# Sample attention on one Trainium2 core: ten key tiles per sequence instead of twelve, a 32-group load for the joined piece of the values, and cached keys that the host lays out turned

## The chip, the cores and the metric

The kernel runs on one core of a Trainium2 chip, as one program. The metric is the device time of one execution in microseconds (us), less is better. A core has five engines that run their own instruction streams (TensorE: PE; VectorE: DVE; ScalarE: ACT; GpSimd: POOL; SyncE: SP, which here only issues DMAs) and 16 DMA engines. The streams meet at semaphores.

## What is computed

One step of a hybrid decoder layer, for a prompt of 2048 tokens and for 8 running sequences of 8 new tokens each (the samples). The change concerns the attention of the samples alone. Each sequence has 2048 cached keys and values (8 heads of 64) and its own 8 new ones:

```python
DILATED = ((128, 1), (512, 4), (2048, 16))

def dilated_attention_sample(q, kc, vc):          # kc, vc: cache and new rows, W = 2048
    for window, dil in DILATED:
        j = jnp.arange(window // dil + 1)
        idx = W + ti[:, None] - dil * j[None, :]   # 129 positions of each token
        kg, vg = kc[:, idx], vc[:, idx]
        s = jnp.einsum('bthd,btjhd->bthj', q, kg)
        mx = jnp.max(s, axis=-1, keepdims=True)
        p = jnp.exp(s - mx)
        ...
    return combine_by_denominator(outs, lses)
```

The three windows are joined by their denominators, which is one softmax in which a position counts once for each window that has it. The kernel does that with one additive mask, the logarithm of the count. Tokens 0 to 7 need, of the cache, the positions whose remainder by 16 is 0 to 7 (over all 2048) and, for the two short windows, positions of the last 512.

## The kernel before

The program has four stages, one after the other with a barrier of all engines between them: `project` (projections), `mix_prompt` (attention and recurrence of the prompt), `mix_sample` (the same for the samples), and `project_out` with `mlp`. The change is in `mix_sample` and in the two places of `mix_prompt` that load keys ahead for it (sequence 0 into `k_first`, sequence 1 into `k_second`).

In `mix_sample` a sequence b has twelve tiles of 128 cached positions, and the 64 new rows of all sequences as a thirteenth (`KT = 13`, `OLD = 12 * P`). Eight tiles are the positions 16i + r, r below 8: partition i gets eight rows of 2 KB that lie together, 16 KB in all. Four tiles are the last 512 positions, four rows or 8 KB in a partition. `load_window` issues the two DMAs of that, for keys (`load_k`, L2023 and L2024) and for values (`load_v`). There are two buffers for the keys (`kin`: `k_first`, `k_second`) and two for the values (`vin`).

Per sequence there are two halves. `first_half(b)`:

- `keys`: TensorE turns each of the twelve tiles, 4 transposes of 128x128 for the four pairs of heads, into one of three PSUM banks (L2469). ScalarE copies the even tiles into `kT` (L2257), VectorE the odd ones (L2326).
- `scores`: for each group of four tiles 4 matmuls with 512 columns of `kT` (L2482), in two PSUM banks by turns, and 4 for the new keys. In the profile a float32 matmul of this kind is two records. The order on TensorE is turn group 0, turn group 1, scores 0, turn group 2, scores 1, scores 2, scores of the new keys.
- `masked`, `maxed` on VectorE add the mask and take the row maximum (L2338, L2344); `exps` on ScalarE takes the exponential over all 1600 columns (L2263).

`second_half(b)`: TensorE turns the probabilities (L2506, L2508), ScalarE and VectorE copy them into `pT` (L2270, L2364, L2366), TensorE multiplies them with the values (13 tiles of 4 matmuls, L2522; called PV below), and VectorE scales the result into `osb` (L2378).

Each engine runs first_half(0), first_half(1), second_half(0), first_half(2), second_half(1), and so on up to second_half(7). Between them lie the recurrence of the samples (a load and a store of its state by POOL's queue, `in_state_C` and `out_C_sample`; its products L2563 and L2532) and the opening of the next stage: loads of `w_out` in four parts (L1802), of `parts` and `mix` (L1806, L1807), their rounding on POOL, ScalarE and VectorE, the first combination on VectorE (`first_weights`, called `between` in second_half(6)), and on TensorE, ahead of PV(7), the products of the first row tile (`first_tile`, L1816 and L292 to L294).

The order of the DMAs is that of SP's stream:

```python
for b in range(DEC_B - 1):
    if b + 2 < DEC_B:
        sp.wait_ge(s["turned"], T.turned("k", b, 11))
        load_k(b + 2)
    if b == 5:
        sp.wait_ge(s["fin"], 16 * 3)
        sp.wait_ge(s["C_out"], 16 * MH)
        ...
        O.load(sp, 0)
        O.load_w(sp, 0)
    if b:
        sp.wait_ge(s["summed"], b)
    load_v(b + 1)
```

After load_v(6) follow the three other parts of `w_out` and O.load(1), then load_v(7). `fin` counts three small stores that SP issues after load_v(5). POOL waits for the turned keys of sequence 0 before it loads the state, and for those of sequence 6 before it rounds `w_out` into the place of `k_first`.

Of the kernel before, what the change touches and what calls it, by code (L numbers as in the profile page):

```python
# [13 lines left out]
P = 128  # L14
# [9 lines left out]
AW = H * HD  # L24
# [1223 lines left out]
def mix_prompt(K):  # L1248
# [12 lines left out]
    with ExitStack() as ctx:  # L1261
# [99 lines left out]
        def _(sp):  # L1361
# [28 lines left out]
            for g in range(T.count + 6):  # L1390
# [27 lines left out]
            sp.wait_ge(s["next_in"], 16 * (2 + SAMPLE_ROWS))  # L1418
# [525 lines left out]
KT = 13  # L1944
OLD = 12 * P
KEYS = OLD + NS
QW = 32


def sample_tables():  # L1950
# [4 lines left out]
    pos = np.concatenate([16 * p + r for r in range(8)] + [WB - 512 + 4 * p + c for c in range(4)]  # L1955
                         + [WB + np.arange(DEC_T)])[None, :]
    back = WB + t - pos
    n = OLD + DEC_T
    part16 = np.zeros(n, bool)
    part16[0:8 * P] = True  # L1960
    new = np.zeros(n, bool)
    new[OLD:] = True
    d16 = (back >= 0) & (back % 16 == 0) & (back <= 2048) & (part16 | new)
    d4 = (back >= 0) & (back % 4 == 0) & (back <= 512) & ~part16
    d1 = (back >= 0) & (back <= 128) & ~part16
# [18 lines left out]
class Turns:  # L1984
# [6 lines left out]
    def __init__(self):  # L1991
        order = [("q", 0, 0), ("new", 0, 0)]
        for b in range(DEC_B + 1):
            if b < DEC_B:
                order += [("k", b, x) for x in range(12)]
# [25 lines left out]

def load_window(sp, dst, cache, b, landed):
    sp.dma_start(dst[:, 0:8], cache[b].rearrange("(i r) c -> i r c", r=16)[:, 0:8]).then_inc(landed, 16)  # L2023
    sp.dma_start(dst[:, 8:12], cache[b, WB - 512:WB, :].rearrange("(i r) c -> i r c", r=4)).then_inc(landed, 16)  # L2024
# [37 lines left out]
def mix_sample(K):  # L2062
# [9 lines left out]
    with ExitStack() as ctx:  # L2072
# [15 lines left out]
        sb("kin_home", [P, 12, AW])  # L2088
        later = [12 * AW]
# [6 lines left out]
        vin = [front("vin0", 12, AW), sb("vin", [P, 12, AW])]  # L2096
        vnew = sb("vnew", [NS, AW])
        kT = sb("kT", [P, 2, PAIRS, 512])
        knT = sb("knT", [P, PAIRS, NS])
        pr = front("pr", 2, KEYS)  # L2100
        qs, knew, mq, mkk, n32 = K.qs, K.knew, K.mq, K.mkk, K.n32
        qz = front("qz", DEC_B, PAIRS, QW)
        pT = front("pT", KT, P)
# [18 lines left out]
        pT_last = kin[1][:].rearrange("p x c -> p (x c)")[:, 12 * AW - KT * P:].rearrange("p (x r) -> p x r", r=P)  # L2122

        def pt(b):
            return pT[:] if b + 1 < DEC_B else pT_last
# [74 lines left out]
        def _(pool):  # L2200
# [15 lines left out]
            pool.wait_ge(s["turned"], T.turned("k", 0, 11))  # L2216
# [12 lines left out]
            pool.wait_ge(s["turned"], T.turned("k", 6, 11))  # L2229
# [5 lines left out]
        def rows(x):  # L2235
            return P if x < 12 else NS

        @block.scalar
        def _(act):
# [11 lines left out]
            def keys(b):  # L2251
                for x in range(0, 12, 2):
                    n = 3 * b + x // 4
                    act.wait_ge(s["turned"], T.turned("k", b, x))
                    if x % 4 == 0 and n >= 2:
                        act.wait_ge(s["scores"], 4 * ((n - 2) // 3) + (n - 2) % 3 + 1)
                    A(kT[:, n % 2, :, P * (x % 4):P * (x % 4 + 1)], bank[T.bank("k", b, x)][:].rearrange("p (h c) -> p h c", h=PAIRS),  # L2257
                      ACT.Copy).then_inc(s["copied_a"], 1)

# [5 lines left out]
            def probs(b):  # L2265
                for i in (0, 2):
# [3 lines left out]
                    A(pt(b)[:, 4 * i:4 * i + 4], bank[T.bank("p", b, i)][:].rearrange("p (x r) -> p x r", x=4),  # L2270
# [15 lines left out]
            keys(0)  # L2286
# [5 lines left out]
            keys(1)  # L2292
            probs(0)
            exps(1)
            for b in range(2, DEC_B):
                keys(b)
# [16 lines left out]
        def _(dve):  # L2313
# [6 lines left out]
            def keys(b, ci):  # L2320
                for x in (4 * ci + 1, 4 * ci + 3):
                    n = 3 * b + ci
                    dve.wait_ge(s["turned"], T.turned("k", b, x))
                    if x % 4 == 1 and n >= 2:
                        dve.wait_ge(s["scores"], 4 * ((n - 2) // 3) + (n - 2) % 3 + 1)
                    v.tensor_copy(kT[:, n % 2, :, P * (x % 4):P * (x % 4 + 1)],  # L2326
                                  bank[T.bank("k", b, x)][:].rearrange("p (h c) -> p h c", h=PAIRS)).then_inc(s["copied_d"], 1)

            def masked(b, c):
                p, n = b % 2, 4 * b + c  # L2330
                w = 512 if c < 3 else NS
# [5 lines left out]
                table = mask[:, 512 * c:512 * (c + 1)] if c < 3 else mask_new[:, b]  # L2337
                v.tensor_tensor_reduce(pr[:, p, 512 * c:512 * c + w], bank[SC[n % 2]][:, 0:w], table, 1.0, 2 * NEG,  # L2338
# [7 lines left out]
            def first_half(b, groups=None):  # L2346
                for ci in range(3):
                    keys(b, ci)
# [9 lines left out]
            def probs(b):  # L2358
                for i in (1, 3):
# [5 lines left out]
                    else:  # L2365
                        ins = v.tensor_copy(pt(b)[0:NS, 12], bank[T.bank("p", b, i)][0:NS, 0:P])  # L2366
# [88 lines left out]
        def _(pe):  # L2455
# [1495 lines left out]
```

## Time and profile before

| | |
|---|---|
| runs | 2785.67, 2789.16, 2790.73 us (median 2789.16) |
| the profiled execution: span from first to last instruction | 2790.8 us |
| the profiled execution: device time | not given apart; its span lies at the upper end of the three runs |
| PE busy | 2667.3 us (96%) |
| DVE, ACT, POOL busy | 1806.6 us (65%), 1075.5 us (39%), 692.4 us (25%) |
| mean granted TensorE clock | 0.986 |
| first instruction of `mix_sample` to its last product | 1076.8 us to 1246.4 us |

Times of the trace are counted from the start of the span. A window row gives, for a stretch, the busy time and number of instructions of each engine, the granted TensorE clock as a share of 2.4 GHz, the busy share of the 16 DMA engines and what they moved.

### The profile page before, as it was taken

The page shows a single profiled execution, that of the slowest core. Times are in us where ns is not written, and L with a number is a line of the kernel's source. Part 1 is how long each engine was busy: PE and PEld are TensorE (multiplying, and loading weights), DVE is VectorE, ACT ScalarE, POOL GpSimd, SP SyncE. Part 2 cuts the span into 40 slices and gives each one's busy share as a digit, 9 for nine tenths or more (in the row PEclk, how much of TensorE's full clock was granted, in tenths as well). Part 3 has the DMA queues.
Part 4 walks back from the last instruction along what each step waited for, and adds up shares of the span by engine and source line. Part 5 has one row for each costly group of instructions (what it writes and reads, how often), then busy time and mean ns, then how long its engine had stood idle before and what let it go on. Part 6 is the DMA issues. An engine that isn't in the chain of part 4 may idle for free. (4 is left out here: it accounts for less than half of the span.)

```text
span 2790.8 us, 45736 instructions
## 1 busy us (share of the span) xinstructions
PE 2667.3 (96%) x17331; PEld 2256.3 (81%) x17331; DVE 1806.6 (65%) x3848; ACT 1075.5 (39%) x1975; POOL 692.4 (25%) x585
## 2 busy tenths in 40 slices
PE   7999999999899998989989999899999999999997
PEld 6888888878777776768877888799998888778886
DVE  6722566333688885567667676755655766887778
ACT  4312332010566774333346555555553211221113
POOL 1167212120245453112210000100002434333332
PEclk9999999999999999989999999999999999999999
DMA  5367543254454547967846777778869777786672
GB/s 184 140 214 265 198 145 143 107 178 139 138 174 155 172 142 290 399 263 261 303 164 209 269 270 269 263 269 298 278 234 335 271 243 255 265 310 225 220 266 87
DMA packets 342705, 628.68 MB, mean 225 GB/s; under 512 B 38431, under 2 KB 241315, under 8 KB 326742
## 3 DMA queue, kind: packets, MB, share of 16 engines
q1 hardware_dynamic: 273132, 530.24, 54.8%
q10 hardware_dynamic: 68218, 91.51, 9.1%
q0 software_dynamic: 1152, 4.19, 0.4%
q8 instruction: 130, 2.13, 0.3%
q14 instruction: 73, 0.60, 0.1%
HBM read 455.36 MB, written 237.61 MB: 248 GB/s over the span
## 5 line engine op out<-in xcount | busy, mean ns | idle before, releaser
L3573 DVE TENSOR_TENSOR mlp_acc<-mlp_acc,bank 128x512 f32<-128x512 f32 x440 | 299.6, 685 | 143.4 <-PE bank L2861 137.1
L2859 PE MATMUL bank<-mlp_wd,mlp_u_hi 128*128 128x512 f32 x896 | 350.5, 391 | 8.9 <-DVE mlp_acc L3573 5.1
L2861 PE MATMUL bank<-mlp_wd,mlp_u_lo 128*128 128x512 f32 x896 | 349.2, 390 | 0.0
L2860 PE MATMUL bank<-mlp_wd,mlp_u_hi 128*128 128x512 f32 x896 | 349.1, 390 | 0.0
L3342 ACT ACTIVATE mlp_u_hi<-mlp_u_raw 128x768 fp32r<-128x768 f32 x126 | 113.1, 945 | 445.4 <-POOL mlp_u_raw L3210 445.0
L2859 PE MATMUL bank<-mlp_h_hi,mlp_wu_hi 128*128 128x272 f32 x896 | 259.3, 289 | 9.3 <-DVE mlp_h_lo L3431 4.8
L2860 PE MATMUL bank<-mlp_h_lo,mlp_wu_hi 128*128 128x272 f32 x896 | 258.8, 289 | 0.0
L2861 PE MATMUL bank<-mlp_h_hi,mlp_wu_lo 128*128 128x272 f32 x896 | 257.9, 288 | 0.0
L292 PE MATMUL p_bank<-p_w_hi,p_hT_hi 128*128 128x512 f32 x640 | 250.4, 391 | 5.2 <-DVE p_stage L836 5.1
L294 PE MATMUL p_bank<-p_w_hi,p_hT_lo 128*128 128x512 f32 x640 | 249.1, 389 | 0.0
L293 PE MATMUL p_bank<-p_w_lo,p_hT_hi 128*128 128x512 f32 x640 | 249.1, 389 | 0.0
L3205 POOL TENSOR_TENSOR mlp_u_raw<-mlp_u_raw 128x256 f32<-128x256 f32 x64 | 50.3, 787 | 718.3 <-DMA mlp_u_raw<-u 718.3
L2859 PEld LDWEIGHTS bank<-mlp_wd,mlp_u_hi 128*128 128x128 f32 x896 | 168.6, 188 | 48.6 <-issue 10.9
L832 DVE TENSOR_TENSOR p_bank<-p_bank,p_rot 128x128 f32<-128x128 f32 x85 | 25.4, 299 | 265.9 <-PE p_bank L294 234.7
L2861 PEld LDWEIGHTS bank<-mlp_wd,mlp_u_lo 128*128 128x128 f32 x896 | 168.5, 188 | 35.3
L2860 PEld LDWEIGHTS bank<-mlp_wd,mlp_u_hi 128*128 128x128 f32 x896 | 168.7, 188 | 34.4
L1508 ACT ACTIVATE mx_probs<-mx_probs,mx_part 128x256 f32<-128x256 f32 (+1 forms) x384 | 143.4, 451 | 96.8 <-DVE mx_part L1587 96.8
L2859 PEld LDWEIGHTS bank<-mlp_h_hi,mlp_wu_hi 128*128 128x128 f32 x896 | 169.4, 189 | 10.7 <-DVE mlp_h_lo L3431 5.7
L2859 PE MATMUL bank<-mlp_g_hi,mlp_wu_hi 128*128 128x512 f32 x444 | 173.4, 391 | 3.7 <-DVE mlp_made L3444 2.1
L2860 PE MATMUL bank<-mlp_g_lo,mlp_wu_hi 128*128 128x512 f32 x448 | 175.3, 391 | 0.0
L2861 PE MATMUL bank<-mlp_g_hi,mlp_wu_lo 128*128 128x512 f32 x444 | 172.8, 389 | 0.0
L2860 PEld LDWEIGHTS bank<-mlp_h_lo,mlp_wu_hi 128*128 128x128 f32 x896 | 169.2, 189 | 0.0
(448 smaller groups left out, 6104.4 us busy)
## 6 DMA issues: line engine op xcount, KB each, us to landing
mlp_wd<-wd SPq DMA_DIRECT2D x31, 2048.0 KB, 8.1
mlp_wd<-wd SPq DMA_DIRECT2D x32, 1536.0 KB, 7.3
mlp_u_raw<-u SPq DMA_DIRECT2D x256, 128.0 KB, 2.4
out_win_k_sample<-in_cache_k SPq DMA_DIRECT2D x48, 680.0 KB, 8.9
out_win_v_sample<-in_cache_v SPq DMA_DIRECT2D x48, 680.0 KB, 9.6
mlp_wu_raw<-in_w_up SPq DMA_DIRECT2D x31, 1024.0 KB, 6.0
p_w_raw<-in_w_tok SPq DMA_DIRECT2D x10, 2048.0 KB
wd<-mlp_un_hi SPq DMA_DIRECT2D x21, 896.0 KB, 4.5
```

Of the source, the lines that this page charges most:

```text
L292: nc.tensor.matmul(out, ah, bh, start=(k == 0), stop=False)
L293: nc.tensor.matmul(out, ah, bl, start=False, stop=False)
L294: ins = nc.tensor.matmul(out, al, bh, start=False, stop=(k == n - 1))
L832: v.tensor_tensor(rot_a, ps[:, :, 0:ROT], tab(0, ROT), ALU.mult)
L1508: ins = A(p_, p_, ACT.Exp, bias=part[a][:, n % 2, 2 * c + e, HD + 1:HW])
L2859: nc.tensor.matmul(out, ah, bh, start=fresh and k == 0, stop=False, skip_group_check=not fresh)
L2860: nc.tensor.matmul(out, ah, bl, start=False, stop=False, skip_group_check=not fresh)
L2861: ins = nc.tensor.matmul(out, al, bh, start=False, stop=k == n - 1, skip_group_check=not fresh)
L3205: g_.tensor_tensor(r[:, 3], r[:, 2], r[:, 5], ALU.add).then_inc(u_sums, 1)
L3342: A(u_hi[b][:, k], u_raw[b][:, k], ACT.Copy).then_inc(u_hi_ready, 1)
L3573: v.tensor_tensor(a, a, b[:], ALU.add).then_inc(summed, 1)
```

## The change

- Tiles: the positions of the last 512 whose remainder by 16 is below 8 are already in the eight first tiles. The four late tiles become two, with remainders 8 to 15 only. `KT` is 11, `OLD` 1280; the mask counts all windows over all columns.
- Values: `load_window` now takes for the late piece, of each 16 rows of the last 512, the second eight: 32 groups of 4 partitions, 2 rows (4 KB) in a partition.
- Keys: the host passes a further input, `cache_kt`, with the keys of the ten tiles turned (for each sequence 128 x 4 x 1280). One DMA brings 20 KB to each partition. `keys` goes on all three engines, the matmuls of `scores` read the loaded buffer itself. The third group of scores has 256 columns.
- What waited for the turned keys of a sequence (SP's next load of keys, POOL's two places) waits for its third group of scores.
- The places of all buffers stay; the mask, the exponential (1344 columns) and the PV (11 tiles) get shorter. The copy of the caches into the outputs still reads `cache_k` and `cache_v`.

```diff
@@ mix_prompt, sync
-                    load_window(sp, K.k_second, K.ins["cache_k"], 1, K.k_second_in)
+                    load_keys(sp, K.k_second, K.ins["cache_kt"], 1, K.k_second_in)
...
-                    load_window(sp, K.k_first, K.ins["cache_k"], 0, s["next_in"])
+                    load_keys(sp, K.k_first, K.ins["cache_kt"], 0, s["next_in"])
@@
-KT = 13
-OLD = 12 * P
+WT = 10
+KT = WT + 1
+OLD = WT * P
@@
+def sample_key_columns(cache):
+
+    p = np.arange(P)
+    late = WB - 512 + 16 * (p // 4) + 8 + 2 * (p % 4)
+    pos = np.concatenate([16 * p + r for r in range(8)] + [late + y for y in range(2)])
+    return cache[:, pos, :].reshape(DEC_B, OLD, H // 2, P).transpose(0, 3, 2, 1)
+
+
+def load_keys(sp, dst, turned, b, landed):
+    sp.dma_start(dst[:], turned[b]).then_inc(landed, 16)
+
 def load_window(sp, dst, cache, b, landed):
     sp.dma_start(dst[:, 0:8], cache[b].rearrange("(i r) c -> i r c", r=16)[:, 0:8]).then_inc(landed, 16)
-    sp.dma_start(dst[:, 8:12], cache[b, WB - 512:WB, :].rearrange("(i r) c -> i r c", r=4)).then_inc(landed, 16)
+    sp.dma_start(dst[:, 8:WT], cache[b, WB - 512:WB, :].rearrange("(i z a y) c -> z i a y c", z=2, a=4, y=2)[1]).then_inc(landed, 16)
@@ mix_sample, sync
-                load_window(sp, kin[b % 2], K.ins["cache_k"], b, k_in[b % 2])
+                load_keys(sp, kin[b % 2], K.ins["cache_kt"], b, k_in[b % 2])
...
-                    sp.wait_ge(s["turned"], T.turned("k", b, 11))
+                    sp.wait_ge(s["scores"], 4 * b + 3)
@@ gpsimd
-            pool.wait_ge(s["turned"], T.turned("k", 0, 11))
+            pool.wait_ge(s["scores"], 3)
...
-            pool.wait_ge(s["turned"], T.turned("k", 6, 11))
+            pool.wait_ge(s["scores"], 4 * 6 + 3)
@@ scalar: keys(b) and its calls go
-            def keys(b):
-                for x in range(0, 12, 2):
...
@@ vector: keys(b, ci) and its call go
-            def keys(b, ci):
-                for x in (4 * ci + 1, 4 * ci + 3):
...
-                w = 512 if c < 3 else NS
+                w = min(512, OLD - 512 * c) if c < 3 else NS
@@ tensor
-            def keys(b, ci):
-                p = b % 2
-                for x in range(4 * ci, 4 * ci + 4):
-                    dst = open_group("k", b, x)
-                    for c in range(PAIRS):
-                        ins = tp(dst[:, P * c:P * (c + 1)], kin[p][:, x, P * c:P * (c + 1)], ident[:])
-                    ins.then_inc(s["turned"], 1)
...
-                w = 512 if ci < 3 else NS
-                if ci < 3:
-                    after(pe, T.out("k", b, 4 * ci + 2))
-                    after(pe, T.out("k", b, 4 * ci + 3))
+                w = min(512, OLD - 512 * ci) if ci < 3 else NS
...
-                    src = kT[:, (3 * b + ci) % 2, c, :] if ci < 3 else knT[:, c, :]
+                    src = kin[b % 2][:, c, 512 * ci:512 * ci + w] if ci < 3 else knT[:, c, :]
```

## Rows read from the trace of the kernel before

**Rows 1.** Span and mean granted TensorE clock of the core.
```profile
core 0: 2790.8 us, clock 0.986
```

**Rows 2.** Windows: stretch, length; PE, PEld, DVE, ACT, POOL busy; clock, DMA share, GB/s.
```profile
1120.00:1140.00 20.00, 19.58 (x246) 16.55 (x243) 13.02 (x36) 6.39 (x10) 0.00 (x0) 1.00 1.00 424
1140.00:1160.00 20.00, 19.58 (x246) 14.84 (x238) 13.37 (x39) 6.69 (x12) 3.75 (x2) 1.00 0.95 381
1180.00:1200.00 20.00, 16.45 (x196) 12.17 (x195) 7.50 (x18) 6.39 (x10) 2.06 (x2) 0.83 1.01 419
```

**Rows 3.** Timeline of TensorE, 1165 to 1224 us: start, length, instruction, [idle before, releaser].
```profile
1165.75 4.49 PE L2522 MATMUL bank<-sm_vin,sm_pT 128*32 128x128 f32 x96 [2.45 <-issue]
...
1205.28 3.88 PE L2469 MATMUL bank<-ident,k_second 128*128 128x128 f32 x32
1209.09 1.07 PE L2482 MATMUL bank<-sm_kT,sm_qz 128*32 128x512 f32 x8
...
1214.16 1.53 PE L2506 MATMUL bank<-ident,sm_pr 128*128 128x128 f32 x12
1215.62 0.43 PE L2508 MATMUL bank<-ident,sm_pr 128*64 128x128 f32 x2
1216.47 2.83 PE L2522 MATMUL bank<-sm_vin,sm_pT 128*32 128x128 f32 x96 [0.42 <-ACT sm_pT L2270]
1219.23 0.42 PE L2522 MATMUL bank<-sm_vnew,sm_pT 64*32 64x128 f32 x8
```

**Rows 4.** Groups of instructions in `mix_sample`: times, busy us, mean ns, idle before.
```profile
L2326 DVE COPY sm_kT<-bank 128x512 f32<-128x512 f32 x48 | 33.1, 691 | 20.0 <-PE bank L2469 19.8
L2257 ACT ACTIVATE sm_kT<-bank 128x512 f32<-128x512 f32 x48 | 28.7, 597 | 51.4 <-PE bank L2469 51.3
```

**Rows 5.** Single DMAs: duration and start of issue, time to landing (keys 3, keys 5, w_out 1 to 3).
```profile
L2024 SPq DMA_DIRECT2D k_second<-in_cache_k x1: 433/433/433, 1099.8 to 1099.8; - x1
...
DMA to landing us min/median/max: 22.6/22.6/22.6
...
L2024 SPq DMA_DIRECT2D k_second<-in_cache_k x1: 432/432/432, 1140.0 to 1140.0; - x1
...
DMA to landing us min/median/max: 11.8/11.8/11.8
...
L1802 SPq DMA_DIRECT2D out_w_raw<-in_w_out x3: 432/442/447, 1189.6 to 1190.6; - x3
...
DMA to landing us min/median/max: 17.0/19.0/21.1
```

**Rows 6.** Windows by what the DMAs carried, and one after a pause of TensorE.
```profile
1078.30:1122.40 44.10, 40.51 (x427) 29.79 (x427) 22.06 (x52) 17.60 (x33) 11.53 (x13) 0.97 1.00 389
1122.40:1151.80 29.40, 28.56 (x396) 23.04 (x393) 19.66 (x56) 10.69 (x18) 3.75 (x2) 1.00 1.00 417
1158.00:1170.30 12.30, 9.85 (x149) 7.56 (x152) 6.76 (x23) 3.06 (x5) 3.57 (x4) 0.86 0.92 338
1165.70:1170.20 4.50, 4.45 (x100) 4.26 (x100) 0.02 (x1) 0.00 (x0) 0.00 (x0) 0.62 0.98 349
```

**Rows 7.** DMA issues, 1050 to 1260 us: times, KB each, median us to landing.
```profile
k_second<-in_cache_k SPq DMA_DIRECT2D x4, 2048.0 KB, 10.5
...
k_second<-in_cache_k SPq DMA_DIRECT2D x4, 1024.0 KB, 12.6
...
out_C_sample<-sm_Cs POOLq DMA_DIRECT2D x4, 512.0 KB, 10.3
```

**Rows 8.** Timeline of all engines, the end of the stage.
```profile
1222.81 0.35 DVE L2378 TENSOR_SCALAR sm_osb<-bank,sm_st 128x128 f32<-128x128 f32 x1
1223.08 0.68 DVE L2364 COPY k_second<-bank 128x512 f32<-128x512 f32 x1
...
1224.05 0.63 PE L1816 MATMUL bank<-ident,out_ma 128*128 128x128 f32 x4 [2.58 <-DVE k_second L2366]
...
1246.04 0.42 PE L2522 MATMUL bank<-sm_vnew,k_second 64*32 64x128 f32 x8
```

More of the change, by code:

```diff
@@ L1941, in sum_up @@
         v.tensor_tensor(w[:, 5], w[:, 4], w[:, 1], ALU.subtract).then_inc(self.wu_t, 1)
-KT = 13
-OLD = 12 * P
+WT = 10
+KT = WT + 1
+OLD = WT * P
 KEYS = OLD + NS
+HOME = 12
 QW = 32
@@ L1954, in sample_tables @@
     p = np.arange(P)
-    pos = np.concatenate([16 * p + r for r in range(8)] + [WB - 512 + 4 * p + c for c in range(4)]
-                         + [WB + np.arange(DEC_T)])[None, :]
+    late = WB - 512 + 16 * (p // 4) + 8 + 2 * (p % 4)
+    pos = np.concatenate([16 * p + r for r in range(8)] + [late + y for y in range(2)] + [WB + np.arange(DEC_T)])[None, :]
+    assert len(set(pos[0].tolist())) == pos.size
     back = WB + t - pos
     n = OLD + DEC_T
[L1959 to L1965, printed above, removed]
+    assert pos.shape[1] == n
+    d16 = (back >= 0) & (back % 16 == 0) & (back <= 2048)
+    d4 = (back >= 0) & (back % 4 == 0) & (back <= 512)
+    d1 = (back >= 0) & (back <= 128)
     count = d16.astype(np.float32) + d4 + d1
@@ L1993, in __init__ @@
         for b in range(DEC_B + 1):
-            if b < DEC_B:
-                order += [("k", b, x) for x in range(12)]
             if b:
@@ L2087, in mix_sample @@
         assert -(-nc.sbuf_base // 32) * 32 == K.front_at + 4 * TOP
-        sb("kin_home", [P, 12, AW])
-        later = [12 * AW]
+        sb("kin_home", [P, HOME, AW])
+        later = [HOME * AW]
         def front(name, *shape):
@@ L2120, in mix_sample @@
         SC, PV, ML = (3, 4), 5, (6, 7)
-        pT_last = kin[1][:].rearrange("p x c -> p (x c)")[:, 12 * AW - KT * P:].rearrange("p (x r) -> p x r", r=P)
+        pT_last = K.place("sm_pT_last", TOP + HOME * AW - KT * P, [P, KT, P])
         def pt(b):
-            return pT[:] if b + 1 < DEC_B else pT_last
+            return pT[:, 0:KT] if b + 1 < DEC_B else pT_last
         def pv(b):
@@ L2235, in rows @@
         def rows(x):
-            return P if x < 12 else NS
+            return P if x < WT else NS
         @block.scalar
@@ L2249, in _ @@
                 act.wait_ge(K.hb_out[p], 16 * (NCH // 2))
-            def keys(b):
-                for x in range(0, 12, 2):
[L2253 to L2258, printed above, removed]
             def exps(b):
@@ L2285, in _ @@
             own.mark(ins)
-            keys(0)
             exps(0)
@@ L2291, in _ @@
             own.mark(ins)
-            keys(1)
             probs(0)
@@ L2295, in _ @@
             for b in range(2, DEC_B):
-                keys(b)
                 probs(b - 1)
@@ L2318, in bc @@
                 return ap.rearrange("p (h a) -> p h a", a=1).broadcast_to([NS, MH, w])
-            def keys(b, ci):
-                for x in (4 * ci + 1, 4 * ci + 3):
[L2322 to L2327, printed above, removed]
             def masked(b, c):
                 p, n = b % 2, 4 * b + c
-                w = 512 if c < 3 else NS
+                w = min(512, OLD - 512 * c) if c < 3 else NS
                 dve.wait_ge(s["scores"], n + 1)
@@ L2336, in masked @@
                     dve.wait_ge(s["turned"], T.turned("p", b - 2, 3))
-                table = mask[:, 512 * c:512 * (c + 1)] if c < 3 else mask_new[:, b]
-                v.tensor_tensor_reduce(pr[:, p, 512 * c:512 * c + w], bank[SC[n % 2]][:, 0:w], table, 1.0, 2 * NEG,
+                at = 512 * c if c < 3 else OLD
+                table = mask[:, at:at + w] if c < 3 else mask_new[:, b]
+                v.tensor_tensor_reduce(pr[:, p, at:at + w], bank[SC[n % 2]][:, 0:w], table, 1.0, 2 * NEG,
                                        ALU.add, ALU.max, st[:, p, c:c + 1]).then_inc(s["masked"], 1)
@@ L2347, in first_half @@
                 for ci in range(3):
-                    keys(b, ci)
                     if ci:
@@ L2486, in first_half @@
                 if b:
-                    pe.wait_ge(k_in[b % 2], 32 * ((b + 1) // 2))
+                    pe.wait_ge(k_in[b % 2], 16 * ((b + 1) // 2))
                 for ci in range(3):
-                    keys(b, ci)
                     if ci:
@@ L2503, in second_half @@
                     if i < 3:
-                        for k in range(4):
+                        for k in range(min(4, WT - 4 * i)):
                             x = 4 * i + k
@@ L2522, in second_half @@
                         ins = mm(bank[pv(b)][QW * c:QW * (c + 1), 0:2 * HD], pt(b)[0:w, x, QW * c:QW * (c + 1)],
-                                 vin[p][:, x, P * c:P * (c + 1)] if x < 12 else vnew[:, P * c:P * (c + 1)],
+                                 vin[p][:, x, P * c:P * (c + 1)] if x < WT else vnew[:, P * c:P * (c + 1)],
                                  start=(x == 0), stop=(x == KT - 1))
@@ L3760, in sb @@
             return ctx.enter_context(K.nc.sbuf_tensor("shared_" + name, shape, F32))
-        K.k_first, K.k_second = K.place("k_first", 0, [P, 12, AW]), K.place("k_second", TOP, [P, 12, AW])
+        K.k_first, K.k_second = K.place("k_first", 0, [P, H // 2, OLD]), K.place("k_second", TOP, [P, H // 2, OLD])
         K.C = sb("C", [P, MH, MD + 1])
```

19 lines of the change are left out of this document (11 added, 8 removed).

## Prediction

> **What bounds the kernel now.** I read the span first [rows 1]: one core, a TensorE clock of 0.986, so there is little disturbance to explain away. The page puts TensorE at 96% of the span, but that is a mean over four stages, and the change touches one. So I next read windows inside `mix_sample` [rows 2]: TensorE is busy 19.58 of 20 us in two of them, and the 16 DMA engines are busy for 0.95 to 1.00 of the same stretches at 381 to 424 GB/s. Two resources look full at once. Which one ends last is seen where a sequence's data lands and where it is used. Keys 3 landed at 1099.8 + 22.6 = 1122.4 us, keys 5 at 1140.0 + 11.8 = 1151.8 us [rows 5]. Part 1 of `w_out` landed at 1189.6 + 17.0 = 1206.6 us [rows 5]; values 6 stand directly ahead of it in SP's queue, so they landed about the 2.5 us of its 1.05 MB before, near 1204, yet PV(6) starts at 1216.47 [rows 3]. So the loads ran some 12 us ahead at the end, and TensorE set the time; but only 12 us ahead. That margin, and not TensorE's share, decides what the change is worth.
>
> **What TensorE loses.** 384 transposes of keys at 3.88 / 32 = 0.121 us [rows 3]: 46.6 us. The third scores group has half its columns: 8 times half of 1.07 us [rows 3], 4.3. Two tiles fewer in the transposes of the probabilities: 16 at 1.53 / 12 = 0.128, 2.0. PV: 8 x 2 tiles x 8 records at 2.83 / 96 = 0.0295 [rows 3], 3.8. Together 56.7 us. ScalarE and VectorE lose 28.7 and 33.1 us of copies [rows 4]; both spent their time waiting for TensorE [rows 4], so this gives nothing by itself. The new waits of SP and POOL on the third scores group come later than the turned keys by about one or two groups of scores, but the scores themselves now start at once: behind SP's wait stand the next keys and values, and those are far back in a full queue anyway.
>
> What is left on TensorE for a sequence: scores 2.5 x 1.07 + 0.3 = 3.0 us, probabilities 1.3 + 0.43 + 0.42 = 2.1, PV 2.4 + 0.4 = 2.8; 7.9 us, plus the recurrence in three of the sequences.
>
> **What the DMAs keep.** A sequence's keys or values are 2048 + 1024 KB = 3.146 MB before [rows 7] and 2560 KB = 2.621 MB after. Keys and values of a sequence need 5.24 MB at 0.42 MB/us = 12.5 us (the window that carries nothing else has 417 GB/s [rows 6]; by the landings of keys 3 and 5, 12.58 MB in 29.4 us, it is 0.428 [rows 5]). That is more than 7.9 us. So the loads become the bound, and the stage is to be summed in bytes:
>
> 1. From load_v(0) at 1078.3 to keys 3. Before: v0, k2, v1, k3 12.58 MB, state 2.10, masks 1.05, rows 0.4, 16.1 MB in 44.1 us, 0.366 MB/us (the window itself has 389 GB/s, since some of values 2 is in it [rows 6]). After: 10.49 + 2.10 + 0.92 + 0.4 = 13.9 MB, 38.0 us: keys 3 land at 1116.3.
> 2. v2, k4, v3, k5, v4, k6, v5, k7: 20.97 MB at 0.42, 49.9 us. Store of the state (4 x 512 KB [rows 7]) and the three small stores, 2.25 MB; where that store ran the rate was 338 GB/s [rows 6], I take 0.36: 6.2 us. Keys 7 land at 1172.4.
> 3. O.load(0), `w_out` 0 and v6: 2.12 + 2.62 MB at 0.42, 11.3 us: values 6 land at 1183.7.
> 4. PV(6) starts there instead of at 1216.5 [rows 3]: 32.8 us earlier.
> 5. From PV(6) on, the tail is the next stage's opening and not bound by sample loads: 30.0 us before, to 1246.5 [rows 8]. Two corrections. VectorE's `first_weights` lay between TensorE's last PV and its own copies of the probabilities, so that TensorE sat idle for 2.58 us before L1816 [rows 8]; now it is done while PV(6) waits for its values: -2.6. And PV(6) starts after a pause. After such a pause of 2.45 us PV(3) took 4.49 us instead of 2.83, at a granted clock of 0.62, partly the lower level of 1.2 GHz [rows 3, 6]. The same factor of 1.6 on PV(6) and on the ten transposes behind it, less their two tiles: +1.9. Net -0.7.
>
> Sum: 32.8 + 0.7 = 33.5 us. 2790.8 - 33.5 = 2757.3 us of span. The profiled execution is 1.6 us over the median of the runs, so 2789.16 - 33.5 = 2755.7, which I round to **2756 us**. The stages behind start from the same state and only shift.
>
> **Is the queue always fed?** At the time when keys b land, v(b-1), k(b+1) and v(b) are issued already, since each waits only for work on sequence b-1 or b-2. The tight place is b = 5: SP waits for `fin`, three small stores queued behind v5, before it issues O.load(0), `w_out` and v6. By the sum v5 lands about 1166 and the stores some 2 us later, while k7 keeps the engines busy to 1172. Margin about 4 us; if it is gone, each us more costs one. In the tail, `w_out` 2 and 3 land 5 and 8 us after v6, O.load(1) 10 us, v7 16 us; they are used some 5, 13, 13 and 26 us after PV(6) starts. Covered, `w_out` 2 just so. The smaller first loads in `mix_prompt` lie under a stage that TensorE orders: 0, with bounds of -1 and +0.5 us.
>
> **Costs that no row shows.** Late values in 32 groups with 4 KB pieces: below, the rate of rows 6 (0.524 MB, 1.25 us); above, the lowest rate there, 338 GB/s (1.55 us), over seven loads +2 us. I take the first, as the same rows of 2 KB come from the same cache. Keys in 20 KB rows from one DMA: they are as long as or longer than any now loaded; the same rate, bounds -0.2 and +1.2 us each (338 GB/s), over the six of the stage -1 to +7. Matmuls reading the loaded buffer instead of `kT`: both are SBUF, 0.
>
> The Trainium skill has a rule that bears on the first of these ("DMA: Bandwidth & Descriptors", section "Why a DMA increments its semaphore by 16 and not by 1", at "How many engines (k)"): a DMA is spread over the largest number up to 16 that divides the slowest dimension of both sides. Here the sides have 32 and 128, which gives 16 and the 1.25 us above; by the four partitions of a group it would be 4. No row of before has this shape.
>
> **Rivals.**
>
> - *TensorE stays the bound, at its lower clock.* Pauses for each sequence might hold it at 1.2 GHz: then the 7.9 us of a sequence become about 15, above the 12.5 of the loads. Over the six sequences from keys 3 on that is 15 us, gain 18, **2771 us**. For it: 0.62 after one pause [rows 6]. Against it: once TensorE is the slower one it has no pauses, and in the windows without pauses the clock is 1.00 [rows 2]. The skill's page "TensorE: Matmul & The Clock Gate" (HAM oscillation) tells of a kernel whose short bursts between DMA waits each began at the low clock; by that this rival would hold. 0.10.
> - *The 32-group load runs on few engines* (the other sign). One engine moves 0.42 / 16 = 0.026 MB/us, so n engines need 20 / n us for a piece instead of 1.25, and the later loads need those engines too. Seven pieces precede PV(6). With four engines +26 us, 2782; with three +38, slower; with one +131, **2887 us**. It decides from 6 us for a piece on. Against it: nothing but the shape, 32 is a multiple of 16. 0.04 for slower, 0.03 for the case of four.
> - *TensorE's saving counts in full*, 57 us, 2732: needs the loads to hide. They can't: 41.9 MB must land before PV(6), at the best 0.428 MB/us 98 us after 1078.3, so PV(6) not before 1176 and the gain not above 41. A better rate in step 1 than the 0.366 gives up to 5 us, near **2750**; 0.10 for below 2751.
> - *The queue runs dry* at b = 5 or at the start: 3 to 8 us, **2762**; 0.08.
>
> **Chances and range.** My forecast, loads as the pace and 2751 to 2761: 0.65. Range 2747 to 2771: above it the few engines (0.07) and part of the low-clock case, below it little. Faster by over 0.2% (which is about what a measurement of this kernel can tell from no change): 0.94; within it 0.01; slower 0.05.
>
> **What would show it.** The DMA share stays at 1.00 from 1078 to past 1185 at 400 GB/s and more, while TensorE's busy share falls to about 0.6 to 0.8 with granted clocks below 1 (right), or stays above 0.9 (the first rival). PV waits on landings of `sm_vin` in most sequences, and PV(6) starts with the landing of values 6, near 1184. TensorE's gap before L1816 is under 1 us. A late-values DMA that lands over 3 us after the piece issued 0.4 us before it shows the second rival. Wrong outright would be a DMA share under 0.9 in the middle with TensorE waiting: then something issues too late.

## The result, and the profile after

The changed kernel took 2770.9 us (median of 4 runs, 2770.26 to 2774.66), the kernel before beside it 2788.56 us (4 runs, 2785.67 to 2790.73). The ratio is 0.994 with a 95% interval of 0.9927 to 0.9954. Measured again later, five runs gave 2770.24 us and 0.9932 (0.9918 to 0.9945). The change makes the kernel faster by 17.7 us, 0.6% (18.8 us in the later series). The forecast was 33 us: the direction held, and about half of the gain is missing.

First the core, as in [rows 1]:

```profile
core 0: 2768.4 us, clock 0.982
```

The windows of `mix_sample` after the change (columns as in [rows 2]; the last one is a short stretch inside the third):

```profile
1080.00:1100.00 20.00, 12.89 (x180) 6.56 (x180) 7.58 (x31) 4.53 (x8) 7.46 (x6) 0.91 1.00 399
1100.00:1120.00 20.00, 7.73 (x50) 7.76 (x51) 0.00 (x0) 0.00 (x0) 0.00 (x0) 0.58 1.02 411
1120.00:1140.00 20.00, 18.72 (x291) 14.48 (x290) 13.18 (x47) 5.05 (x10) 3.74 (x2) 1.00 0.72 274
1140.00:1160.00 20.00, 16.77 (x219) 10.67 (x221) 13.00 (x49) 4.26 (x7) 3.57 (x4) 0.91 1.00 401
1160.00:1180.00 20.00, 13.61 (x245) 7.29 (x237) 5.63 (x21) 2.86 (x6) 0.00 (x0) 0.91 1.02 422
1180.00:1200.00 20.00, 9.20 (x116) 7.53 (x116) 17.79 (x22) 5.38 (x8) 13.63 (x4) 0.71 1.01 419
...
1122.00:1127.00 5.00, 4.54 (x103) 3.70 (x102) 4.00 (x12) 2.38 (x4) 0.00 (x0) 1.00 0.08 28
```

As forecast, the DMA engines are full and TensorE isn't: 12.89, then 7.73 of 20 us. But from 1120 to 1140 the roles are reversed again: TensorE is busy for 18.72 us and the DMA share is 0.72 at 274 GB/s, where before it was 1.00 at 424 [rows 2]. From 1122 to 1127 the DMA engines are nearly idle, at 28 GB/s. The prediction had named a DMA share under 0.9 in the middle as what would prove it wrong. It had added "with TensorE waiting"; here TensorE's long wait lies just before the hole (1097.8 to 1112.3 us), not in it.

TensorE's timeline shows what stands ahead of that hole, and the end of the stage (start, length, instruction, idle before with its releaser):

```profile
1112.27 9.46 PE L2541 MATMUL bank<-sm_Cs,sm_qm 128*64 128x129 f32 x64 [14.49 <-DMA sm_Cs<-in_state_C]
...
1175.48 3.72 PE L2461 MATMUL bank<-k_second,sm_qz 128*32 128x512 f32 x24 [4.61 <-DMA k_second<-in_cache_kt]
...
1186.70 4.49 PE L2500 MATMUL bank<-sm_vin,sm_pT 128*32 128x128 f32 x80 [5.08 <-DMA sm_vin<-in_cache_v]
...
1199.23 1.09 PE L1816 MATMUL bank<-ident,out_ma 128*128 128x128 f32 x4 [5.66 <-DVE sm_pT_last L2356]
...
1221.25 0.42 PE L2500 MATMUL bank<-sm_vnew,sm_pT_last 64*32 64x128 f32 x8
```

Two waits were not in the forecast: 14.49 us for the recurrence's state at L2541 (which is L2563 of before), and 5.66 us before L1816, where it had said under 1 us. Keys 7 and values 6 are waited for (4.61 and 5.08 us), which fits the loads as the pace, and PV(6) then takes 4.49 us, as PV(3) did after its pause before [rows 3]. One sign did not come: PV was to wait for its values in most sequences, and it did so in two, PV(5) for 1.12 us and PV(6).

**The first loss: the state.** The kernel before issued the state's load later and yet did not wait for it:

```profile
L2218 POOL DMA_DIRECT2D sm_Cs<-in_state_C x4: 882/887/1067, 1087.8 to 1090.7; - x4
...
DMA to landing us min/median/max: 12.0/18.6/26.3
```
```profile
1117.07 7.23 PE L2563 MATMUL bank<-sm_Cs,sm_qm 128*64 128x129 f32 x64 [1.25 <-DMA sm_Cs<-in_state_C]
```

The same load after the change:

```profile
L2228 POOL DMA_DIRECT2D sm_Cs<-in_state_C x4: 882/887/1067, 1080.3 to 1083.1; - x4
...
DMA to landing us min/median/max: 13.8/20.9/29.0
```

It was issued 7.5 us earlier, but its last part landed at 1083.1 + 29.0 = 1112.1 us, only 5 us earlier than before (1090.7 + 26.3 = 1117.0), and 4.1 us of that is the whole stage, whose load_v(0) was issued at 1074.19 instead of 1078.34 us. TensorE, with no keys to turn, was there at 1112.27 - 14.49 = 1097.8 us; before it came at 1115.8. The DMA queues of 1080 to 1112 us say why the landing takes so long (packets, MB, share of the 16 engines' time; the first is SP's queue, the second POOL's):

```profile
q1 hardware_dynamic: 889, 10.63, 82.4%
q0 software_dynamic: 576, 2.10, 18.0%
```

POOL's 2.10 MB go beside 10.63 MB of SP's queue and get less than a fifth of the engines. The Trainium skill ("DMA: Bandwidth & Descriptors", section "Queues, rings and completion order") says that each DMA engine takes turns between its queues packet by packet; the trace fits that only roughly, since it isn't one for one: 576 packets against 889, of 3.6 KB against 12 KB.

The wait would be harmless by itself, with the loads as the pace. What counts stands behind it. In TensorE's stream PV(1) comes after the state's products, and SP's load_v(3) waits for PV(1). SP's own issues in the stretch (start, length):

```profile
1092.84 0.33 SPq L2033 DMA_DIRECT2D sm_vin<-in_cache_v  x1
1093.21 0.59 SPq L2034 DMA_DIRECT2D sm_vin<-in_cache_v  x1
1097.30 0.33 SPq L2029 DMA_DIRECT2D k_first<-in_cache_kt  x1
```
```profile
1126.66 0.33 SPq L2033 DMA_DIRECT2D sm_vin<-in_cache_v  x1
```

For 29 us nothing is issued. Keys 4, the last in the queue, are reported landed at 1097.3 + 26.5 = 1123.8 us; the window from 1122 us on shows that next to nothing is moved any more, and the queue is dry until load_v(3).

**The second loss: the end of the stage.** VectorE and POOL, 1182 to 1199 us:

```profile
1182.49 4.51 POOL L1854 TENSOR_TENSOR out_w_lo<-out_w_raw,out_w_hi 128x2048 fp32r<-128x2048 f32 x1
1182.67 4.39 DVE L1868 TENSOR_TENSOR out_st<-out_st,out_pt 128x24 f32<-128x24 f32 x1
...
1191.57 4.84 POOL L1854 TENSOR_TENSOR out_w_lo<-out_w_raw,out_w_hi 128x2048 fp32r<-128x2048 f32 x1
1192.07 4.89 DVE L1892 TENSOR_TENSOR out_prod_first<-out_prod_first 128x512 f32<-128x512 f32 x1
...
1198.26 0.68 DVE L2354 COPY sm_pT_last<-bank 128x512 f32<-128x512 f32 x1
```

VectorE's sum over 24 columns took 4.39 us and ended 0.06 us after the POOL subtraction beside it; its sum over 512 columns took 4.89 us and ended 0.55 us after POOL's, which is about its own length. Before, the same two took:

```profile
1216.69 0.20 DVE L1868 TENSOR_TENSOR out_st<-out_st,out_pt 128x24 f32<-128x24 f32 x1
...
1221.09 0.69 DVE L1892 TENSOR_TENSOR out_prod_first<-out_prod_first 128x512 f32<-128x512 f32 x1
```

POOL's two subtractions had been done by 1213.3 us then. That is 4.2 + 4.2 us on VectorE (and 1.7 more, since its three products between them took 3.59 us beside POOL's cast instead of 1.90), and its copies of the last probabilities, for which TensorE waits, stand behind. The Trainium skill has this ("SBUF — State Buffer", section "SBUF: two separate sides"): a VectorE operation with two inputs in SBUF and a GpSimd operation that reads SBUF need the same pair of ports, and the one that comes first has it for its whole length. The rows agree: VectorE isn't slowed in proportion to its own work. Each sum ends when POOL's instruction is over, or its own length after that.

### The profile page after: what moved, and what is told of

Same layout as the page of the kernel before. It is cut to its first block and busy times, and to the rows that moved or that the text cites. A ratio compares the mean times of both kernels' runs of the same rounds, so it can differ in the third digit from the quotient of the medians.

```text
span 2768.4 us, 44506 instructions
## 1 busy us (share of the span) xinstructions
PE 2615.6 (94%) x16803; PEld 2209.4 (80%) x16803; DVE 1780.3 (64%) x3800; ACT 1045.1 (38%) x1927; POOL 685.4 (25%) x585
## 5 line engine op out<-in xcount | busy, mean ns | idle before, releaser
L3320 ACT ACTIVATE mlp_u_hi<-mlp_u_raw 128x768 fp32r<-128x768 f32 x126 | 113.1, 946 | 446.6 <-POOL mlp_u_raw L3188 446.2
```

Source lines behind the costliest of these rows:

```text
L3320: A(u_hi[b][:, k], u_raw[b][:, k], ACT.Copy).then_inc(u_hi_ready, 1)
```

## The experiments

All ratios are against the kernel before, in the same series; after a median stand its runs' extremes. Since one execution differs from another by some us, the stretch itself was also read from each kernel's timeline, of one execution each:

| kernel | load_v(0) to PV(6), us | PV(6) to the end of PV(7) | both |
|---|---|---|---|
| before | 1078.34 to 1216.47: 138.1 | 30.0 | 168.1 |
| changed | 1074.19 to 1186.70: 112.5 | 35.0 | 147.5 |
| changed, again | 1074.18 to 1187.26: 113.1 | 35.0 | 148.1 |
| the prediction | 105.4 | 29.3 | 134.7 |
| ten tiles alone | 1077.81 to 1197.80: 120.0 | 32.4 | 152.4 |
| turned keys alone | 1076.52 to 1205.16: 128.6 | 34.2 | 162.8 |
| late values plain | 1075.94 to 1189.02: 113.1 | 35.3 | 148.4 |
| state on SP's queue | 1075.65 to 1181.30: 105.7 | 35.0 | 140.6 |
| products behind PV(1) | 1073.15 to 1181.98: 108.8 | 35.0 | 143.8 |
| state at the stage's start | 1079.39 to 1184.48: 105.1 | 35.5 | 140.6 |
| the last two together | 1072.56 to 1182.57: 110.0 | 35.0 | 145.0 |
| POOL's rounding later | 1071.82 to 1182.40: 110.6 | 32.1 | 142.6 |
| it and products behind PV(1) | 1075.19 to 1183.92: 108.7 | 32.8 | 141.6 |
| it and state on SP's queue | 1077.49 to 1183.72: 106.2 | 33.8 | 140.0 |

### The parts of the change

**Ten tiles alone**, the kernel before with these edits (the scores, masks and copies shortened to match, the keys still turned on TensorE):

```diff
-KT = 13
-OLD = 12 * P
+WT = 10
+KT = WT + 1
+OLD = WT * P
@@ load_window
-    sp.dma_start(dst[:, 8:12], cache[b, WB - 512:WB, :].rearrange("(i r) c -> i r c", r=4))
+    sp.dma_start(dst[:, 8:WT], cache[b, WB - 512:WB, :].rearrange("(i z a y) c -> z i a y c", z=2, a=4, y=2)[1])
```

> Ten tiles and the 32-group load of the late values, keys still turned on TensorE. Theory (TensorE sets the time of the kernel before and its loads run only 12 us ahead): each sequence loses 2.2 us of TensorE work (8 transposes of 0.121 us, half a scores group 0.53, two probability transposes 0.25, two tiles of PV 0.47), 17.8 us over eight; some 5 us of it go back because the state load still lands near 1115 us while TensorE comes to it earlier. 2773 to 2779 us, so most of what the whole change gave. Rival (the host's turning is what gave the gain): 2783 us or more.

Measured: 2773.41 us (2770.22 to 2776.46), ratio 0.9948 (0.9935 to 0.9961). In its windows TensorE stays busy, and by 1140 us the DMA share has room:

```profile
1100.00:1120.00 20.00, 19.19 (x242) 15.55 (x243) 7.77 (x25) 5.36 (x9) 0.00 (x0) 1.00 1.00 398
...
1140.00:1160.00 20.00, 17.45 (x249) 13.55 (x242) 13.57 (x42) 5.75 (x12) 3.76 (x5) 1.00 0.84 307
```

About three quarters of the measured gain is there with the tiles alone: 13.5 us by the medians, of 17.7 and 18.8.

The trace of this kernel shows one thing more. TensorE still turns the keys, and yet it waits 5.05 us before L1816, since VectorE's first combination already meets POOL's subtraction (its first sum, over 8 columns, ends with POOL's instruction at 1201.04 us):

```profile
1196.49 4.55 POOL L1854 TENSOR_TENSOR out_w_lo<-out_w_raw,out_w_hi 128x2048 fp32r<-128x2048 f32 x1
...
1197.62 3.45 DVE L1866 TENSOR_TENSOR out_st<-out_pt 128x8 f32<-128x8 f32 x1
```

**Turned keys alone**, the changed kernel with twelve tiles:

```diff
-WT = 10
+WT = 12
@@ sample_key_columns
-    late = WB - 512 + 16 * (p // 4) + 8 + 2 * (p % 4)
-    pos = np.concatenate([16 * p + r for r in range(8)] + [late + y for y in range(2)])
+    pos = np.concatenate([16 * p + r for r in range(8)] + [WB - 512 + 4 * p + c for c in range(4)])
```

> Keys turned by the host, but twelve tiles for keys and values as before. Theory (the loads are the pace once TensorE does not turn keys): 6.9 MB more have to land before PV(6) than in the changed kernel, 16 us at 0.42 MB/us, so about 2783 to 2790 us, hardly faster than before although TensorE loses 47 us of work; DMA share near 1.00 through the stage. Rival (TensorE's work counts, the changed kernel was held up only by single waits): 47 us less work shows for at least half, 2765 us or less.

Measured: 2786.18 us (12 runs, 2780.91 to 2791.06), ratio 0.9997 (0.9987 to 1.0008): taking the transposes of the keys from TensorE is worth at most some 4 us by the interval while the loads are as long as before. Its one trace has the stretch to PV(6) shorter by 9.5 us and the end of the stage longer by 4.2. TensorE's longest single waits in the stage (in total, times, longest) are for loads:

```profile
PE bank L2542 <- DMA sm_Cs<-in_state_C: 7.9, 1, 7.9
PE bank L2462 <- DMA k_first<-in_cache_kt: 6.7, 1, 6.7
```

So the tiles shorten both resources and bring most of the gain; the host's turning takes work only from TensorE, and by itself gives next to nothing. It isn't the bytes alone that hold this kernel: the DMA share is 0.79 from 1140 to 1160, so here too loads are issued too late. What the turning is worth depends on that: on top of ten tiles it gives 3 us as the change has it, and 10 us once the load of the state is repaired (2763.67 below, against 2773.41).

**The late values as one plain group.** It settles what the 32 groups cost:

```diff
-    sp.dma_start(dst[:, 8:WT], cache[b, WB - 512:WB, :].rearrange("(i z a y) c -> z i a y c", z=2, a=4, y=2)[1])
+    sp.dma_start(dst[:, 8:WT], cache[b, WB - 256:WB, :].rearrange("(i y) c -> i y c", y=2))
```

> The changed kernel, but the late values come from the last 256 positions, two rows in each of 128 partitions, one plain group (other values than the attention needs; bytes and pieces of 4 KB are the same). Theory (the 32-group form costs nothing by itself: alone it landed 1.2 us behind the large piece): 2769 to 2773 us. Rival (32 groups are spread badly over the engines, over 1 us for each piece): 2763 us or less.

Measured: 2770.3 us (2764.84 to 2776.5), ratio 0.9933 (0.9908 to 0.9957), the same as the changed kernel. In the changed kernel the grouped piece of values 3, issued into the empty queue at 1127.0, landed after 8.2 us, the 2 MB piece issued at 1126.7 after 7.3: 1.2 us apart. In this one the times are 1127.9 + 8.4 and 1127.6 + 7.5, again 1.2 us apart. The prediction's 1.25 us stands, and with it the Trainium skill's rule that was put beside it: 0.524 MB in 1.2 us is the rate of all the engines together. The kernels' times could not decide this alone, with an interval of 7 us to either side; the landings do.

### The state's wait

**The state on SP's queue**, behind values 1, so that it has no second queue beside it:

```diff
@@ sync, behind load_v(b + 1)
+                if b == 0:
+                    by_head = Cs[:].rearrange("p (b h) c -> p b h c", h=MH)
+                    for h in range(MH):
+                        sp.dma_start(by_head[:, :, h, 0:MD], K.ins["state_C"][:, h].rearrange("b d e -> d b e")).then_inc(s["C_in"], 16)
@@ gpsimd: the same four DMAs and their wait for scores 3 go
```

> The changed kernel with the load of the recurrent state issued by SP behind values 1 instead of by POOL. Theory (the state load in POOL's own queue gets about a fifth of the engines' packets beside SP's full queue, lands 29 us after its issue, and TensorE waits 14.5 us for it; in that wait SP issues no new load and the queue runs dry for 4.6 us): it lands in the order in which it is needed, some 6 us behind values 1; TensorE waits under 8 us, the queue never runs dry, values 6 land 4 to 6 us earlier, 2764 to 2767 us. Rival (all is bytes, the order of the loads does not matter): 2770 to 2772 us.

Measured: 2763.67 us (2761.5 to 2766.05), ratio 0.9917 (0.9903 to 0.9931). TensorE still waits 9.9 us for the state, more than the 8 forecast, but the window with the hole is full, and the landing is quicker:

```profile
1120.00:1140.00 20.00, 19.17 (x269) 13.42 (x263) 15.67 (x56) 2.67 (x6) 3.74 (x2) 1.00 1.00 411
```
```profile
L2193 SPq DMA_DIRECT2D sm_Cs<-in_state_C x4: 604/2480/12641, 1083.3 to 1100.1; - x4
...
DMA to landing us min/median/max: 7.0/13.5/19.5
```

**The products moved behind PV(1)**, on TensorE and, for the numerators, on VectorE. The load stays as it is:

```diff
@@ tensor
-            pe.wait_ge(s["act_ml"], 3)
-            ... the wait for C_in and the 64 products
             second_half(1)
+            pe.wait_ge(s["act_ml"], 3)
+            ... the same
@@ vector
-            second_half(1, numerators)
+            second_half(1)
+            numerators()
```

> The changed kernel with the products of the state moved behind second_half(1) on TensorE, and their sums on VectorE too. The state load stays in POOL's queue and lands as late. Theory (what costs is not TensorE's wait but that PV(1) stands behind it, so that SP's load of values 3 is held back and the queue runs dry): the wait stays, the DMA share has no hole near 1122 to 1127 us, 2764 to 2767 us. Rival (TensorE's wait of 14.5 us itself is the loss): 2770 to 2772 us, since the wait is as long.

Measured: 2764.77 us (2762.97 to 2774.17), ratio 0.9929 (0.9912 to 0.9946). The state lands as late as ever (14.5/21.1/29.1 us after its issue), but only 2.26 us are waited for it, so the wait did not stay as the forecast had it, and the rival's condition wasn't met:

```profile
1120.00:1140.00 20.00, 17.07 (x209) 11.93 (x210) 15.83 (x56) 2.67 (x6) 3.75 (x2) 1.00 0.86 350
```
```profile
1110.85 8.89 PE L2543 MATMUL bank<-sm_Cs,sm_qm 128*64 128x129 f32 x64 [2.26 <-DMA sm_Cs<-in_state_C]
```

The hole is smaller and has moved. Values 3 are now issued at 1108.6 us, but the scores of sequence 3 stand behind the products, and SP's load of keys 5 waits for those: it issues nothing from 1109.6 to 1129.5 us.

```profile
1126.00:1132.00 6.00, 5.55 (x64) 3.75 (x67) 5.32 (x22) 1.81 (x3) 3.09 (x2) 1.00 0.55 174
```

One kernel keeps a wait of 9.9 us and one of 2.3 us, and the one with the long wait is no slower: 105.7 us to PV(6), against 108.8 and the changed kernel's 112.5. What counts is how full the window with the hole gets (411, 350 and 274 GB/s), so it is the load held back that costs, and not TensorE's wait. By ratio the gains on the changed kernel (mean of its two, 0.9936) are 5 and 2 us, the second within the noise.

**The state issued by POOL at the stage's start**, without its wait for the scores of sequence 0:

```diff
@@ gpsimd
             g.memset(qm[:], 0.0).then_inc(s["clear"], 1)
+            for h in range(MH):
+                pool.dma_start(by_head[:, :, h, 0:MD], K.ins["state_C"][:, h].rearrange("b d e -> d b e")).then_inc(s["C_in"], 16)
...
-            pool.wait_ge(s["scores"], 3)
-            for h in range(MH): ... the same DMAs
```

> The changed kernel with POOL's load of the state issued at once at the stage's start, behind POOL's three clears, instead of after the scores of sequence 0: some 4 to 5 us earlier. Theory (about a fifth of the packets beside SP's queue, so some 25 us from issue to landing whenever it is issued): it lands 4 to 5 us earlier, TensorE's wait and the hole in the loads shrink by that, 2766 to 2768 us. Rival (it takes its share from keys 2 and values 1, which were late already): 2770 us or more.

Measured: 2763.4 us (2759.23 to 2767.12), ratio 0.9905 (0.9888 to 0.9922), 3 us below the expected range, with 105.1 us to PV(6). The state's wait shrinks, and part of it turns up as a wait for keys 2, which now share the engines with the state; the hole is gone:

```profile
1120.00:1140.00 20.00, 18.72 (x289) 13.68 (x288) 15.23 (x53) 5.05 (x10) 3.75 (x2) 1.00 1.01 423
```
```profile
PE bank L2460 <- DMA k_first<-in_cache_kt: 7.1, 1, 7.1
...
PE bank L2540 <- DMA sm_Cs<-in_state_C: 2.7, 1, 2.7
```

**Two of these together, and the changed kernel again.** The first of these kernels has both edits of the two diffs just shown (early load, products behind PV(1)).

> The state is loaded at the stage's start (alone: 2763) and its products stand behind the PV of sequence 1 (alone: 2765). Theory (both only keep the values' loads from being held back by the state, and the loads are the pace): they don't add, 2761 to 2765; the DMA share stays near 1.00 from 1080 to 1180. Rival (each takes away a wait of its own, 7 and 6 us): they add, 2757 to 2759.

> The changed kernel once more, unedited, beside the two kernels of this call, so that gains of 3 to 8 us over it are read against runs of the same chip. Both theories: 2771 us, ratio 0.993 to 0.995, TensorE's wait for the state near 14 us and its gap before L1816 over 5 us.

Measured: 2765.66 us (2761.92 to 2768.79), ratio 0.9919 (0.9905 to 0.9933), beside the changed kernel's 2770.24 us (2766.21 to 2771.23), 0.9932 (0.9918 to 0.9945). The repairs don't add; with 110.0 us to PV(6) the two are not even as good as the early load alone (105.1). The trace shows part of the reason: as with the products moved alone, SP issues nothing from 1107.8 to 1126.8 us, since keys 5 wait for the scores behind the products, and from 1124 to 1130 the DMA engines move 320 GB/s, with TensorE busy throughout at a granted clock of 0.50, the lower level of 1.2 GHz. How much of the 5 us this explains wasn't tested. The unedited kernel repeats its picture closely, 14.69 us for the state, 5.53 us before L1816, 265 GB/s from 1120 to 1140.

### The end of the stage

**POOL rounds `w_out` only once VectorE's first combination is done:**

```diff
@@ gpsimd
             pool.wait_ge(s["scores"], 4 * 6 + 3)
+            pool.wait_ge(O.mixed, 1)
```

> The changed kernel, but POOL waits for VectorE's first combination before it rounds w_out. Theory (in the changed kernel the two fall together, and two of VectorE's instructions that read two buffers take 4.4 and 4.9 us instead of 0.2 and 0.7, each as long as POOL's 4.5 us subtraction; TensorE waits 5.7 us for what follows on VectorE): both are short again, TensorE's wait before L1816 falls under 1 us, 4 to 5 us faster, 2765 to 2768 us. Rival (the wait comes back as a wait of the products for w_out, since POOL ends 7 us later): 2770 to 2774 us.

Measured: 2769.85 us (2761.49 to 2773.73), ratio 0.9935 (0.9919 to 0.9951): about 1 us better than the changed kernel, which isn't clear of the noise. The forecast of 4 to 5 us missed, and the rival's range is nearer. The profiled execution is the fastest of the six (2761.49 us), so the trace flatters this kernel. In the trace the collision is gone and the wait before L1816 with it, and both come back behind it:

```profile
1178.11 0.20 DVE L1868 TENSOR_TENSOR out_st<-out_st,out_pt 128x24 f32<-128x24 f32 x1
...
1181.98 0.69 DVE L1892 TENSOR_TENSOR out_prod_first<-out_prod_first 128x512 f32<-128x512 f32 x1
...
1191.95 4.53 POOL L1854 TENSOR_TENSOR out_w_lo<-out_w_raw,out_w_hi 128x2048 fp32r<-128x2048 f32 x1
...
1193.45 5.18 DVE L1854 TENSOR_TENSOR out_w_lo<-out_w_raw,out_w_hi 128x2048 fp32r<-128x2048 f32 x1
```
```profile
1189.91 0.63 PE L1816 MATMUL bank<-ident,out_ma 128*128 128x128 f32 x4 [0.42 <-ACT sm_pT_last L2273]
...
1196.54 0.80 PE L292 MATMUL bank<-out_w_hi,out_mT_hi 128*128 128x512 f32 x1 [1.10 <-POOL out_w_lo L1854]
...
1203.59 0.50 PE L292 MATMUL bank<-out_w_hi,out_mT_hi 128*128 128x512 f32 x1 [1.64 <-DVE out_w_lo L1854]
```

From the start of PV(6) to the end of PV(7) it is 32.1 us, against 35.0 in the changed kernel. The forecast's 29.3 plus these two waits (1.10 + 1.64) gives 32.0. So the wait of 5.66 us is freed, and half of it goes back at once.

**This together with the products moved:**

> Both repairs: the products of the state behind second_half(1), and POOL's rounding behind VectorE's first combination. Theory (two separate losses, the first 6 us by its own run, the second 4 to 5): 2759 to 2762 us. Rival (they cover each other): as the first alone, 2764 us or more.

Measured: 2768.24 us (2761.51 to 2770.43), ratio 0.9925 (0.9908 to 0.9942): a miss, the rival's range came. TensorE waits 4.4 us for the low parts of `w_out` (0.7 for POOL's, 3.7 for VectorE's), and the stretch from PV(6) to PV(7) is 32.8 us. The trace, again of the fastest execution, shows 2 us less there than with the products alone; the runs show no difference (ratio 0.9929 there).

**And together with the state on SP's queue:**

> The state loaded by SP's queue behind values 1 (alone: 2764) and GpSimd's rounding of w_out held until VectorE's first combination is done (alone: 2770, 1 us less than the changed kernel). Theory (the second repair gives its time back as a wait for the low part of w_out, as with the products moved, 2768): 2762 to 2766. Rival (the end of the stage still holds some 3 us that a repair without the low part's lateness would free): 2760 or less.

Measured: 2762.21 us (2761.16 to 2763.28), ratio 0.9906 (0.989 to 0.9921). All its runs lie below all of the changed kernel beside it (2766.21 to 2771.23), by 8 us in the medians. It is the fastest median of all, though by ratio level with the state at the stage's start (0.9905); against the state on SP's queue alone (2763.67, 140.6 us of stretch against 140.0) nothing is resolved.

## Why the prediction came out half right

| | predicted | measured |
|---|---|---|
| load_v(0) to keys 3 (step 1) | 38.0 us | 1074.2 to 1111.5: 37.3 |
| keys 3 to keys 7 (step 2) | 56.1 | 1111.5 to 1175.4: 63.9 |
| keys 7 to PV(6) (step 3) | 11.3 | 1175.4 to 1186.7: 11.3 |
| PV(6) to the end of PV(7) (step 5; 30.0 before) | 29.3 | 1186.70 to 1221.67: 35.0 |

Keys 3 and 7 are from their loads (1087.3 + 24.2 and 1158.0 + 17.4 us).

**What held.** The loads become the pace of the stage: DMA share 1.00 or more in five of the six windows from 1080 to 1200, TensorE waiting for keys and values, clocks of 0.58 to 0.91 where it waits. Steps 1 and 3 came out within 0.7 us. The slow PV(6) came too, a little dearer than costed: 4.49 us for 80 records, where 1.6 times the 2.83 us less two tiles is 4.1. The 32-group load cost its 1.25 us, and of the rival in which TensorE stays the bound at its lower clock (2771 us) only the number was hit: where that clock is low, TensorE waits, as with 0.58 from 1100 to 1120 beside a DMA share of 1.02.

**Step 2 failed, by 7.8 us, through "Is the queue always fed?".** The prediction said that v(b-1), k(b+1) and v(b) are issued already when keys b land, and looked for the tight place at b = 5. The tight place was b = 2: load_v(3) waits for PV(1), and PV(1) stands behind the state's products. The wait for the state was not in the sum at all, since the kernel before hid all but 1.25 us of it behind the turning of the keys. What had hidden it was TensorE's own work, and the change removed it. The DMA share below 0.9 in the middle is the sign that the prediction had set for this; with the state on SP's queue, or loaded at the stage's start, the stretch to PV(6) was 105.7 and 105.1 us, where the prediction had 105.4. Step 2 itself, from keys 3 to keys 7, was 56.9 and 55.9 us in these two, against 56.1 predicted: its bytes and rates were right, and the issue of the loads was what failed. By size it is the rival "the queue runs dry, 3 to 8 us", at another place than the two that it named.

**Step 5 failed, by 5.7 us.** "-2.6, `first_weights` is done while PV(6) waits for its values" took VectorE's durations as fixed. It did begin ahead of that PV (1181.9 us), but so did POOL's rounding, which the landing of `w_out` 0 at 1180.4 us released. Before, POOL began it at 1197.9 us and was done 3 us before VectorE began its combination at 1216.3 us. Now VectorE's combination stands behind the landing of keys 7 (1175.4 us) and POOL's rounding behind the next pieces of the same queue, so they meet. That TensorE turns keys 7 would not keep them apart: with ten tiles alone it does, and they meet as well (5.05 us before L1816). The two-input sums were blocked, 4.2 us twice, and the wait before L1816 became 5.66 us, not under 1. With POOL held back it was 0.42 us: the step's own reasoning was right but for the engine beside it. That this frees only about half of it in the trace, and nothing clear of the noise in the runs, was not foreseen either: POOL's and VectorE's low parts of `w_out` are late next.

**The sum.** 33.5 - 7.1 (load_v(0) to PV(6): 112.5 us against 105.4) - 5.7 = 20.7 us by the two traces from load_v(0) to PV(7): before 1078.34 to 1246.46, 168.1 us; after 1074.19 to 1221.67, 147.5. The medians say 17.7 and 18.8 in the two series; the remaining 2 to 3 us lie within what one execution differs from another (the kernel before ran from 2780.7 to 2798.5 us in all). Repairing the first loss gave 5 and 9 us by ratio, repairing both 8 us and not 13, so the price of the second loss stays a reading of traces (5.7 us) that no run confirms. Of the 5.3 us that the best kernel's stretch is over the prediction (140.0 against 134.7), 4.0 are TensorE's waits for the low parts of `w_out` (1.45 and 2.50 us); the rest wasn't separated. One reading of the prediction was loose without touching the 33.5 us: it took the profiled execution to be 1.6 us over the median by comparing a span with a device time, and in the later runs of the kernel before the device time is 2.4 to 3.1 us longer than the span.

## What to carry to other kernels

When a change moves the bound from an engine to the loads, follow every wait of the issuing queue back through the engine's stream: a wait that cost nothing as long as the engine was late (here 1.25 us for the state) now stands ahead of what the loads wait for, and its price is about the time for which the queue is dry (some 5 us, with 7 lost in all), not its own length (14.5 us). DMAs on a second queue beside a full one land as that queue leaves them room, here 2.1 MB in about 29 us; issuing them earlier, or on the full queue at the right place, kept them from holding back what comes after. Moving the waiting work behind the next load only moved the hold to the load after that (keys 5). And where work is pulled forward into a gap, look what else is released at about that time, by the same event or by the next load in the queue; two engines that never met before may meet there.

## What the runs showed of the hardware

- The load of the state, 2.1 MB in 512 KB parts on POOL's queue, took 23.6 to 29.6 us at the longest from issue to landing beside SP's full queue in eleven traces (26.3 before, 29.0 after, 29.6 with turned keys alone, 23.6 with the tiles alone); on SP's queue 19.5 and 20.2 us. The pieces differ too: on POOL's queue the 2.1 MB are 576 packets; with them on SP's queue that queue has 5041 packets from 1080 to 1112 us, instead of 889.
- Issuing took longer when much was queued already: in the kernel with the state on SP's queue one DMA took 12.6 us to issue and the four together 18.33 us, and in the changed kernel the main piece of values 7 took 4.26 us, where that of values 3, issued into an empty queue, took 0.33. Whether bytes or packets fill the queue isn't shown.
- A VectorE sum with both inputs in SBUF was held until POOL's subtraction beside it was over, whatever its size: 3.45 us instead of 0.15 (8 columns), 4.39 instead of 0.20 (24 columns), 4.89 instead of 0.69 (512 columns). POOL's own subtraction grew only from 4.55 to 4.84 us.
